# Gated feed-forward on one Trainium2 core: another order of GpSimd's sums, deeper buffers and held weights in the down projection, and its token tiles in groups of two, three and three

## The reference, cut to what matters

```python
def conv_glu(h, up, conv, down):
    z = dwconv3(h @ up, conv)                 # [1024, 5632], three taps along the tokens
    gate, val = jnp.split(z, 2, -1)
    return (jax.nn.gelu(gate, approximate=True) * val) @ down
# in each layer, after the mixer:
h = rmsnorm(x, norm_g[l, 2]) * (1.0 + sc2) + sh2
y = conv_glu(h, ffn_up[l], ffn_conv[l], ffn_down[l])
x = x + gt2 * rmsnorm(y, norm_g[l, 3])
```

## Time and profile before

| | |
|---|---|
| runs shown, us | 3122.65, 3127.65, 3120.7 (median 3122.65) |
| profiled execution, us | 3122.5 |
| its span, first to last instruction | 3120.7 us |
| TensorE matmuls busy | 2678.5 us, 86% of the span |
| VectorE, ScalarE, GpSimd busy | 51%, 37%, 31% |
| mean granted TensorE clock | 0.932 of full speed |

### The profile page before, as it was taken

One profiled execution on the slowest core, in us unless ns is written; L12 is line 12 of the kernel. 1 busy time (PEld: TensorE's weight loads), 2 busy tenths in 40 slices (PEclk: granted clock), 3 DMA queues, 4 the chain that ended last, 5 costly groups with the idle time before them and its releaser, 6 DMA issues. The chain is left out here.

```text
span 3120.7 us, 55117 instructions
## 1 busy us (share of the span) xinstructions
PE 2678.5 (86%) x23104; PEld 2150.6 (69%) x23104; DVE 1596.7 (51%) x2273; ACT 1141.6 (37%) x1794; POOL 973.0 (31%) x660
## 2 busy tenths in 40 slices
PE   2698997964899999376999999998776999999997
PEld 1576775621898898155877777876555877777886
DVE  4463564504555553426455555445626455556445
ACT  2211215433343342233433333446333333333444
POOL 0411211003121120232577773000131577774000
PEclk9899998976999999678999999999878999999999
DMA  4554744055313110332222225565032222224566
GB/s 164 162 195 166 239 155 140 16 201 193 84 44 84 44 44 3 136 122 81 72 80 79 79 80 166 174 198 194 29 109 89 63 79 80 81 81 166 182 215 192
DMA packets 304733, 371.62 MB, mean 119 GB/s; under 512 B 31973, under 2 KB 227906, under 8 KB 304494
## 3 DMA queue, kind: packets, MB, share of 16 engines
q1 hardware_dynamic: 294846, 361.87, 35.9%
q10 hardware_dynamic: 9648, 6.34, 0.6%
HBM read 292.61 MB, written 75.55 MB: 118 GB/s over the span
## 5 line engine op out<-in xcount | busy, mean ns | idle before, releaser
L2366 POOL TENSOR_TENSOR cg_u_lo<-cg_u_raw,cg_u_hi 128x512 fp32r<-128x512 f32 x216 | 328.0, 1527 | 211.1 <-ACT cg_u_hi L2257 211.1
L304 PE MATMUL cg_ps<-m_hi,cg_u_hi 128*128 128x512 f32 x768 | 300.6, 391 | 31.0 <-POOL cg_u_lo L2366 31.0
L304 PE MATMUL cg_ps<-over_f_d_hi,cg_a_hi 128*128 128x512 f32 x704 | 279.2, 397 | 28.5 <-DVE cg_a_lo L2429 27.3
L305 PE MATMUL cg_ps<-m_lo,cg_u_hi 128*128 128x512 f32 x768 | 300.1, 391 | 0.0
L306 PE MATMUL cg_ps<-m_hi,cg_u_lo 128*128 128x512 f32 x768 | 299.9, 391 | 0.0
L2257 ACT ACTIVATE cg_u_hi<-cg_u_raw 128x512 fp32r<-128x512 f32 x216 | 131.8, 629 | 451.2 <-PE cg_ps L306 249.7
L2427 DVE TENSOR_TENSOR over_f_d_lo<-over_f_d_raw,over_f_d_hi 128x1024 fp32r<-128x1024 f32 x132 | 163.8, 1241 | 240.9 <-ACT over_f_d_hi L2291 240.7
L305 PE MATMUL cg_ps<-over_f_d_lo,cg_a_hi 128*128 128x512 f32 x704 | 276.0, 392 | 0.0
L306 PE MATMUL cg_ps<-over_f_d_hi,cg_a_lo 128*128 128x512 f32 x704 | 276.0, 392 | 0.0
L2291 ACT ACTIVATE over_f_d_hi<-over_f_d_raw 128x1024 fp32r<-128x1024 f32 x132 | 139.8, 1059 | 240.1 <-PE cg_ps L306 218.7
L2413 DVE SCALAR_TENSOR_TENSOR cg_z<-cg_ps,top_conv_f,cg_z 128x1023 f32<-128x1023 f32 x88 | 112.9, 1283 | 180.1 <-ACT cg_z L2281 180.1
(11 more groups left out here) (368 smaller groups left out, 5974.0 us busy)
## 6 DMA issues: line engine op xcount, KB each, us to landing
over_f_d_raw<-in_ffn_down SPq DMA_DIRECT2D x132, 512.0 KB
cg_u_raw<-in_ffn_up SPq DMA_DIRECT2D x88, 512.0 KB, 4.8
za_mw<-in_ada_w SPq DMA_DIRECT2D x12, 2048.0 KB
scr_act<-cg_z SPq DMA_DIRECT2D x44, 512.0 KB, 2.6
cg_a_raw<-scr_act SPq DMA_DIRECT2D x88, 192.0 KB
qkv_mw<-in_ada_w SPq DMA_DIRECT2D x8, 2048.0 KB
mod_w<-in_ada_w SPq DMA_DIRECT2D x8, 1024.0 KB
za_w_raw<-in_mix_in SPq DMA_DIRECT2D x16, 512.0 KB, 4.3
```

Of the source, the lines that this page charges most:

```text
L304: nc.tensor.matmul(out, a_hi, b_hi, start=first, stop=False)
L305: nc.tensor.matmul(out, a_hi, b_lo, start=False, stop=False)
L2366: G.tensor_tensor(u_lo[:, n % RING], source(g, i), u_hi[:, n % RING].bitcast(F32), ALU.subtract).then_inc(ulo_done, 1)
```

## The change

In the up phase, GpSimd forms the first two sums of a group ahead of `low(g, 0)`. The two halves of `u_raw` have semaphores of their own, and the value half is loaded first. In the down phase the groups are (0, 1), (2, 3, 4), (5, 6, 7). There are seven raw buffers (`RAWS`; the new ones lie in `u_raw`, `u_s`, `m1`, `u2`, `u3`) and three split ones (in `u_hi[0]`, `u_lo[0]` and the feature tensors `h_hi`, `h_lo`, which are free once the up phase's matmuls are done). The split weights of the five blocks in `KEPT` stay in `h_lo` and `h_hi` over all passes, and are loaded and split once. Loads, residual rows and stores are issued at other places, and the copies out of PSUM stand behind split part `k` = 1 instead of `k` = 0.

```diff
-GROUPS = ((0, 1, 2), (3, 4, 5), (6, 7))
+GROUPS = ((0, 1), (2, 3, 4), (5, 6, 7))
+KEPT = (3, 7, 11, 15, 19)
...
+        SPLITS = [q for q in range(NQ) if q < FT or q % FT not in KEPT]
+        RINGED = [q for q in range(NQ) if q % FT not in KEPT]
+        kept = [h_lo[:, j, :] for j in range(KT)] + [h_hi[:, j, :] for j in range(HK, KT)]
...
-                for x in range(2):
-                    sp.dma_start(u_raw[:, g % 2, x], up_v[g + x * FT]).then_inc(u_loaded[g % 2], 16)
+                for x in (VAL, GATE):
+                    sp.dma_start(u_raw[:, g % 2, x], up_v[g + x * FT]).then_inc(u_loaded[g % 2][x], 16)
...
             def load_part(q):
-                if q >= 3:
-                    sp.wait_ge(dlo_done, q - 2)
-                    sp.wait_ge(alo_done, q - 2)
                 tiles, k = part_of(q)
-                sp.dma_start(d_raw[:, q % 3, :], down_v[k]).then_inc(d_loaded[q % 3], 16)
+                if q in SPLITS:
+                    j = SPLITS.index(q)
+                    if j >= RAWS:
+                        sp.wait_ge(dlo_done, j - RAWS + 1)
+                    sp.dma_start(d_raws[j % RAWS], down_v[k]).then_inc(d_loaded[j % RAWS], 16)
+                if q >= RAWS:
+                    sp.wait_ge(alo_done, q - RAWS + 1)
...
             store_act(NG - 2)
-            for q in range(3, 6):
+            sp.wait_ge(ulo_done, ITEMS)
+            if PLAIN < NG:
+                sp.wait_ge(c12_done, NG - PLAIN)
+            for q in range(3, RAWS):
                 load_part(q)
             store_act(NG - 1)
             sp.wait_ge(umm_done, ITEMS)
-            for t in range(4):
-                tail.load_x(sp, t)
-            tail.load_rows(sp)
-            if follows:
-                tail.load_columns(sp)
-            for q in range(6, NQ):
+            for q in range(RAWS, NQ):
                 load_part(q)
                 p, k = divmod(q, FT)
+                if p == 0 and k in (9, 12, 15, 18):
+                    tail.load_x(sp, (k - 9) // 3)
+                if q == 20:
+                    tail.load_rows(sp)
...
             def split_part(q):
-                if q >= 2:
-                    after(act, q - 2)
+                if q == 2:
+                    act.wait_ge(umm_done, ITEMS)
+                if q >= 3:
+                    after(act, q - 3)
...
-                if k == 0 and p:
+                if k == 1 and p:
                     for i, t in enumerate(GROUPS[p - 1]):
                         act.wait_ge(tile_done, t + 1)
                         A(y[:, t, :], slots[i], ACT.Copy).then_inc(evicted, 1)
...
-                low(g, 0)
-                pool.wait_ge(ulo_done, n + 1)
+                for x in range(2):
+                    pool.wait_ge(u_loaded[g % 2][x], 16 * (g // 2 + 1))
+                pool.wait_ge(ulo_done, n)
                 G.tensor_tensor(u_s[:, :, :], raw(g, VAL, 0), raw(g, VAL, 1), ALU.add).then_inc(s_done, 1)
                 pool.wait_ge(s_done, m + 1)
                 G.tensor_tensor(raw(g, VAL, 0), raw(g, GATE, 0), raw(g, VAL, 0), ALU.subtract).then_inc(s_done, 1)
+                low(g, 0)
                 pool.wait_ge(s_done, m + 2)
+                pool.wait_ge(ulo_done, n + 1)
                 G.tensor_tensor(raw(g, GATE, 0), u_s[:, :, :], raw(g, GATE, 0), ALU.subtract).then_inc(s_done, 1)
```

More of the change, by code:

```diff
@@ L2180, in part_of, with weights, splits_to @@
             return GROUPS[q // FT], q % FT
+        SPLITS = [q for q in range(NQ) if q < FT or q % FT not in KEPT]
+        RINGED = [q for q in range(NQ) if q % FT not in KEPT]
+        kept = [h_lo[:, j, :] for j in range(KT)] + [h_hi[:, j, :] for j in range(HK, KT)]
+        def weights(q):
+            if q % FT in KEPT:
+                j = KEPT.index(q % FT)
+                return kept[2 * j], kept[2 * j + 1]
+            j = RINGED.index(q) % 3
+            return (d_hi[:, j, :], d_lo[:, j, :]) if j < 2 else (kept[2 * len(KEPT)], kept[2 * len(KEPT) + 1])
+        d_raws = [d_raw[:, j, :] for j in range(3)] + [u_raw[:, j, x].rearrange("p t c -> p (t c)") for j in range(2) for x in range(2)]
+        a_raws = [a_raw3[:, j, :] for j in range(3)] + [flat(u_s), m1, u2, u3]
+        a_his = [a_hi2[:, 0, :], a_hi2[:, 1, :], flat(u_hi[:, 0])]
+        a_los = [a_lo2[:, 0, :], a_lo2[:, 1, :], flat(u_lo[:, 0])]
+        def splits_to(q):
+            return sum(1 for r in SPLITS if r <= q)
         def after(eng, q):
@@ L2209, in load_part @@
                 n = len(tiles) * P
-                sp.dma_start(a_raw[:, q % 3, 0:n], act_d[k, :, tiles[0] * P:tiles[0] * P + n]).then_inc(a_loaded[q % 3], 16)
+                sp.dma_start(a_raws[q % RAWS][:, 0:n], act_d[k, :, tiles[0] * P:tiles[0] * P + n]).then_inc(a_loaded[q % RAWS], 16)
             load_up(0)
@@ L2227, in _ @@
             sp.wait_ge(umm_done, ITEMS)
-            for t in range(4):
-                tail.load_x(sp, t)
-            tail.load_rows(sp)
-            if follows:
-                tail.load_columns(sp)
-            for q in range(6, NQ):
+            for q in range(RAWS, NQ):
                 load_part(q)
                 p, k = divmod(q, FT)
+                if p == 0 and k in (9, 12, 15, 18):
+                    tail.load_x(sp, (k - 9) // 3)
+                if q == 20:
+                    tail.load_rows(sp)
+                    if follows:
+                        tail.load_columns(sp)
                 if p:
                     for i, t in enumerate(GROUPS[p - 1]):
-                        if k == 8 + 5 * i:
+                        if k == 11 + 5 * i:
                             tail.store_x(sp, t)
-                            if t + 4 < TT:
-                                tail.load_x(sp, t + 4)
+                        if k == min(13 + 5 * i, FT - 1) and t + 4 < TT:
+                            tail.load_x(sp, t + 4)
             for t in GROUPS[-1]:
@@ L2425, in split_part @@
                 n = len(part_of(q)[0]) * P
-                dve.wait_ge(dhi_done, q + 1)
-                V.tensor_tensor(d_lo[:, q % 2, :], d_raw[:, q % 3, :], d_hi[:, q % 2, :].bitcast(F32), ALU.subtract).then_inc(dlo_done, 1)
+                if q in SPLITS:
+                    j = SPLITS.index(q)
+                    w_hi, w_lo = weights(q)
+                    dve.wait_ge(dhi_done, j + 1)
+                    V.tensor_tensor(w_lo, d_raws[j % RAWS], w_hi.bitcast(F32), ALU.subtract).then_inc(dlo_done, 1)
                 dve.wait_ge(ahi_done, q + 1)
-                V.tensor_tensor(a_lo[:, q % 2, 0:n], a_raw[:, q % 3, 0:n], a_hi[:, q % 2, 0:n].bitcast(F32), ALU.subtract).then_inc(alo_done, 1)
+                V.tensor_tensor(a_los[q % 3][:, 0:n], a_raws[q % RAWS][:, 0:n], a_his[q % 3][:, 0:n].bitcast(F32), ALU.subtract).then_inc(alo_done, 1)
             if PLAIN < NG:
@@ L2557, in down @@
                 tiles, k = part_of(q)
-                pe.wait_ge(dlo_done, q + 1)
+                w_hi, w_lo = weights(q)
+                pe.wait_ge(dlo_done, splits_to(q))
                 pe.wait_ge(alo_done, q + 1)
                 for i, t in enumerate(tiles):
-                    if q < FT and k == 0:
+                    if k == 0 and (q < FT or i >= len(GROUPS[q // FT - 1])):
                         pe.wait_ge(conv_done, 2 * NG - 1 if i == 2 else 2 * (NG - 1))
```

34 lines of the change are left out of this document (19 added, 15 removed).

## The result

The changed kernel takes 3081.68 us in the median (3079.66 to 3083.65, four runs), the kernel before 3122.9 (3120.7 to 3127.65, four runs beside them): a ratio of 0.9866, 95% interval 0.9849 to 0.9883. Its profiled execution took 3079.66 us, with a span of 3077.9. The forecast was 3084.

The account below looks back on a forecast made before the run. TensorE was taken as the bound in all four phases. Up phases -22.3, down phases with tails -10.1 and -9.5 and clock +3.4 gave -38.5 us from 3122.65, forecast 3084 us, 8-in-10 range 3072 to 3102.

Parts of the forecast that it names:

- end of layer 0: Layer 0's tail after its last down matmul: three tiles instead of two follow the last step, +7.6 us.
- GpSimd's order: Up phases: two sums run in GpSimd's waiting time, so TensorE's stall in each group goes; -22.3 us in sum.
- The value half first: Start of each up phase: GpSimd's first low part still ends late beside VectorE's two-operand subtraction; gain 0.
- the bound of -1.8: Other end of the range for loading the value half first, at each layer's up phase start: -1.8 us per layer.
- The start of the down phase: Step 2 is wanted earlier, but its weights' low part stays behind the last group's second convolution: 3.5 us lost per layer.
- The passes: Steady down passes: three split buffers suffice; layer 0 keeps feature stalls of 1.87 us three times and 0.4 once.
- The held weights' 0: Down passes: held weights save five of 22 splits in two passes, off the path with the deeper ring; gain 0.
- The clock: Down phases: new idle time of 3.4 us may halve the clock; 1.7 us taken in each layer, +3.4.
- Rival 1: First down pass: DMA becomes the bound at about 245 GB/s, +8.5 us in each layer, 3101 us; chance 0.12.
- Rival 2: Up phase: the stall only moves, item 0's low part coming late; 22 us less gain, 3106 us; chance 0.06.
- rival 3: Up phase: VectorE blocks GpSimd's five close operations, 3.8 us in 38 groups, slower at 3230 us; chance 0.03.
- rival 4: More gain: first low part ahead of VectorE (-3.6), clock stays (-3.4), turn's stalls shrink by 3; 3074 us; chance 0.09.

Follow-up runs that it names:

- up phase only: The kernel before with only the up phase's edits (GpSimd's two sums ahead of its low part, value half first, own semaphores): 3104.9 us, ratio 0.9944.
- Low first: The changed kernel with one wait more on VectorE, so its third sum over features waits for GpSimd's first low part: 3082.15 us, one run.
- Parts first: The changed kernel with down parts 2 and 3 split ahead of the last gate and last gelu, part 3 loaded earlier: 3078.81 us, one run.
- the other four edits: Changed kernel with later features, earlier splits of parts 2 and 3, woven tail, VectorE's third sum behind GpSimd's low part: 3064.49 us; with old groups 3057.62 us.

## Why the prediction was right

The terms as forecast and as measured, in us (for the whole program 3084 against 3081.68):

| term | forecast | measured |
|---|---|---|
| up phase, layers 0 and 1 | -22.3 in sum | -10.2, -11.7 |
| start of the up phase | 0, 0 | -2.2, 0 |
| down phase of layer 0, with the clock | -16.0 | -16.1 |
| end of layer 0 | +7.6 | +7.8 |
| down phase of layer 1, with the clock | -9.1 | -11.0 |
| end of layer 1 | +1.3 | +1.3 |
| stages outside the change | 0 | -1.4, +0.8 |
| sum (the measured one from unrounded times) | -38.5 | -42.8 |

The profiled executions differ by 4.3 us more than the forecast said, the medians by 2.7 (41.2 against 38.5). Of the 4.3, 2.2 are the start of layer 0's up phase and 1.7 layer 1's clock, and both are shown below to fall either way from one kernel to the next.

**GpSimd's order.** Right in mechanism and size: all stalls gone, and "up phase only" shows that they go by this edit. Layer 0's 427.0 us instead of 426 are the earlier start, whose first 5.5 us ran at half clock, against 3.5 before.

**The value half first.** Right in layer 1, wrong in layer 0, by a race. These are the rows of layer 0's start:

```profile
1472.41 0.63 ACT L2287 ACTIVATE cg_u_hi<-cg_u_raw 128x512 fp32r<-128x512 f32 x1 [7.72 <-DMA cg_u_raw<-in_ffn_up]
1473.12 1.26 POOL L2401 TENSOR_TENSOR cg_u_lo<-cg_u_raw,cg_u_hi 128x512 fp32r<-128x512 f32 x1 [4.56 <-ACT cg_u_hi L2287]
1473.15 3.37 DVE L2438 TENSOR_TENSOR m_f<-m_f 128x2048 f32<-128x2048 f32 x1
...
1474.43 0.80 PE L304 MATMUL cg_ps<-m_hi,cg_u_hi 128*128 128x512 f32 x1 [13.51 <-POOL cg_u_lo L2401]
```

GpSimd came 0.03 us ahead of VectorE, took 1.26 us, and VectorE's sum took 3.37 instead of 2.29. In layer 1 it came 0.08 us behind, and TensorE began 3.39 us after it. The prediction put a single outcome on a start that lies within 0.1 us of the other engine's; the bound of -1.8 was about the size (-2.2), and 1.0 of it went back through the clock. "Low first" sets the order and shows the cause. The other kernels show that it is a race: nine have this program at the start of the up phase (the changed one and the eight made without an added wait on VectorE there), and ahead of layer 0's first matmul TensorE was idle for 13.4 to 13.5 us in four of them and for 15.70 in five, in layer 1 for 13.0 to 13.1 in three and for 15.26 in six. In the three with the wait it was 13.6 to 13.7 and 13.1 to 13.3. So the 0 of the forecast was the more frequent outcome, and the -2.2 of layer 0 chance. The Trainium skill's rule that the later of the two waits in full (SBUF — State Buffer, Who interferes with whom) agrees with these rows in both directions; it doesn't tell who will be first.

**The start of the down phase.** 3.00 us idle for the 3.5 lost that were forecast (3.2 from start to start), at the same step in both layers, and no wait behind the residual rows. "Parts first" shows the cause named in the prediction, the split of part 2 behind the last group's second convolution.

**The passes.** No wait elsewhere in layer 1; in layer 0 three of 1.69 us and one of 0.24, where 1.7 three times and 0.4 once were forecast. Both kernels that move the features or the scaling remove them, so the chain on VectorE is the cause. The working in the prediction, features, scaling and sum in a row on VectorE ahead of the split, is what its rows show. The held weights' 0 holds within 0.4 us.

**The clock.** The step that failed in layer 1. Forecast were +1.7 in each layer; the clock fell to its lower level (1.2 instead of 2.4 GHz) in layer 0,

```profile
1910.10:1913.40 3.30, 3.30 (x8) 2.62 (x9) 3.30 (x4) 2.05 (x4) 0.00 (x0) 0.50 1.01 394
```

and not in layer 1, after the same wait. In the changed kernel and the six made from it that keep this wait, it fell in five of seven in layer 0 and three of seven in layer 1. A term that comes in half of the cases should have gone into the range with half its size, not into the sum twice.

**The rivals.** Rival 1 (DMA at 245 GB/s) is out: the last row shows 394 GB/s at a share of 1.01, and in the first pass of the changed kernel TensorE waited for no load. Rival 2 and rival 3 are out: TensorE waits for no low part within the up phases, and GpSimd's mean times are those of before but for the two sums shown above, in one group of each layer. Of rival 4 about half came: the low part slipped in first in layer 0, and the clock stayed in layer 1; the turn's stalls did not shrink.

**What the prediction did not see** is that the groups cost more than they give. It had both terms (+7.6 and +1.3 at the ends, 2.7 at step 2 in each layer) but never set them against the old groups with the new buffers: 11 us by the medians, of which the ends are 9.0, and 6.9 us once the other four edits are in.
